# Sums of squares of two RMS norms: added on GpSimd instead of TensorE, and half blocks of the products that may be parted in their middle

## The chip, the cores and the metric

The kernel runs on 1 core of a Trainium2 chip. The metric is the time of the device in microseconds (us), the median of 3 runs; less is better. TensorE is PE in the profile, its weight loads are PEld, VectorE is DVE, ScalarE is ACT, GpSimd is POOL, SyncE (which issues most DMAs) is SP.

## What is computed

One step of a decoder layer, for 1024 prompt tokens and 32 sample tokens that share all weights (1056 columns in all). The part that the change touches comes after the mixer's recurrences and ahead of the MLP:

```python
h = h + rmsnorm(merged @ w_out, norm_mix_post)
xa = cross_attend(rmsnorm(h, norm_xa_pre), mk, mv, xa_wq, xa_wo)
h = h + rmsnorm(xa, norm_xa_post)
ff = square(relu(rmsnorm(h, norm_mlp_pre) @ mlp_w1)) @ mlp_w2
h = h + rmsnorm(ff, norm_mlp_post)

def rmsnorm(x, g):       # x: tokens x 1024, all in float32
    return x * rsqrt(mean(x * x, -1) + 1e-6) * g
def cross_attend(xn, k, v, w_q, w_o):   # 4 heads of 256, 256 memory tokens
    q = xn @ w_q
    return softmax(q . k / 16) . v @ w_o
```

## The kernel before

The last block of the program (`back`) holds features on the 128 partitions (8 blocks of 128 features) and tokens along the free axis, in three chunks of 288, 384 and 384 tokens, in this order. It multiplies by four 1024x1024 matrices in turn (`BackProducts`): the mixer's last branch, w_out, xa_wq, xa_wo. That makes 12 stretches (matrix, chunk), numbered kk = 0 to 11, each of 8 products; a product is two halves of 12 matmuls, since each float32 factor is split into a high and a low part and three of the four partial products are taken (4 input blocks x 3). The high part of a half's weights is made by ACT (`high`, L3163), the low part by DVE (`low`, L3169), three halves ahead.

Two norms follow each of the stretches kk = 3, 4, 5 (w_out) and kk = 9, 10, 11 (xa_wo): `BackNorms`. Here these six are called norm chunks 0 to 5; chunks 0 and 3 have 288 tokens, the others 384. For each:

- Norm 1: of each of the 8 blocks of the product, ACT copies it out of PSUM (L3329) and squares it into one of two buffers `sq` (L3333); PE multiplies the squares by a matrix of ones, which sums over the 128 features of the block and over the blocks in PSUM (`tensor`, L3368). Then ACT makes 1/sqrt as an Ln (L3340) and an Exp (L3342).
- DVE scales two blocks (L3387, twice) and adds the residual (L3390), four times: that gives the new h.
- Norm 2: ACT squares each block of the new h into one of two buffers `sq2` (L3352), PE sums (`tensor2`, L3375), Ln and Exp again, DVE scales (L3396), ACT and DVE split the result into high and low (L3359, L3404). This runs beside the next stretch's products, or, for chunk 5, beside the first products of the MLP (`BackMlp`, L3810), whose order is: four blocks of weights, each with tokens 768-1055 and then 0-383, then the same four with tokens 384-767, which are chunk 5's.

In the stretches 7 and 8 the attention of the prompt (`PromptAttention`: scores L3459, transposes L3471, mixing L3480) and of the samples (`SampleAttention`: transposes of the keys L3602, scores L3611, mixing L3621) is put between the halves.

The order on each engine is set when the program is written. Each piece of work is a generator that yields the time at which its next instructions are due, by a plan (`BackTimes`: for a half 12 x (0.000417 x tokens + 0.012) us, and some room per stretch), and `weave` always takes the piece that is due first. The engines then run in that order and wait for semaphores. So a position in the order is a position in the plan, and the chip can be ahead of it or behind it.

Of the kernel before, what the change touches and what calls it, by code (L numbers as in the profile page):

```python
# [22 lines left out]
KD = D // P  # L23
# [999 lines left out]
class RwkvMasks:  # L1023
# [32 lines left out]
    def pool(self, pool):  # L1056

        def keep(at, pattern, base, mult):
            pool.affine_select(out=at, in_=at, compare_op=ALU.is_ge, fill=0.0, base=base, pattern=pattern, channel_multiplier=mult)
            return pool.drain()  # L1060

        def blocks(t):
            return t.rearrange("p (a c) -> p a c", c=16)
        yield 1
        pool.wait_ge(self.ones_made, 1)
        keep(blocks(self.within), [[-16, 8], [0, 16]], 0, 1)
        keep(blocks(self.within), [[16, 8], [0, 16]], 15, -1)
# [2057 lines left out]
class BackProducts:  # L3125
# [45 lines left out]
    def multiply(self, pe, ready):  # L3171
        for hu, u, hf, b, raw in self.halves():
            yield self.times.half(hu)
            kk = u // 8
            t0, m = self.times.CHUNKS[kk % 3]
            if b == 0:
                for sem, n in ready[kk][hf]:
                    pe.wait_ge(sem, n)
            pe.wait_ge(self.w_lo, hu + 1)
            if hf == 0 and u >= 2:  # L3180
                pe.wait_ge(self.off[u % 2], u // 2)
            ps = self.bank(u)[:, 0:m]
            for q in range(4):
                for i, (w, x) in enumerate(((self.hi, 0), (self.hi, 1), (self.lo, 0))):
                    last = self.nc.tensor.matmul(ps, w[:, hu % 4, q, :], self.pair[x][:, 4 * hf + q, t0:t0 + m],  # L3185
                                                 start=hf == 0 and q == 0 and i == 0, stop=hf == 1 and q == 3 and i == 2)
            last.then_inc(self.product if hf else self.used, 1)
# [95 lines left out]
class BackNorms:  # L3283


    def __init__(self, k, ctx, products, gains):
        self.k, self.nc, self.pr, self.times, self.pair, self.gains = k, k.nc, products, products.times, products.pair, gains
        S = lambda n: k.sem(f"bn_{n}")
        (self.h_in, self.h_out, self.squared, self.summed, self.squared2, self.summed2, self.rstd1, self.resid, self.rstd2, self.normed, self.n_hi, self.n_lo) = (
            S(n) for n in ("h_in", "h_out", "squared", "summed", "squared2", "summed2", "rstd1", "resid", "rstd2", "normed", "n_hi", "n_lo"))  # L3290
        self.sq, self.sq2 = [ctx.enter_context(k.nc.sbuf_tensor(f"bn_sq{i}", [P, 2, 384], F32)) for i in range(2)]
        self.rstd = ctx.enter_context(k.nc.sbuf_tensor("bn_rstd", [P, 384], F32))

# [25 lines left out]
    def evacuate(self, act, work_free):  # L3319
        for i, s, kk, t, m, end in self.items():  # L3320
            for b in range(8):
                u = 8 * kk + b
                yield self.times.off(u)
                if b == 0:
                    sem, n = work_free[kk]
                    act.wait_ge(sem, n)
                act.wait_ge(self.pr.product, u + 1)
                ps = self.pr.bank(u)[:, 0:m]
                self.nc.scalar.activation(self.work[kk % 2][:, b, 0:m], ps, ACT.Copy)  # L3329
                n = 8 * i + b  # L3330
                if n >= 2:
                    act.wait_ge(self.summed, n - 1)
                self.nc.scalar.activation(self.sq[:, n % 2, 0:m], ps, ACT.Square).then_inc(self.squared, 1)  # L3333
                act.drain().then_inc(self.pr.off[u % 2], 1)

    def scalar(self, act):
        activation = self.nc.scalar.activation
        for i, s, kk, t, m, end in self.items():
            def root(bank, done):
                activation(self.rstd[:, 0:m], bank[:, 0:m], ACT.Ln, bias=self.k.eps[:, 0:1], scale=1.0 / D)  # L3340
                act.drain()
                activation(self.rstd[:, 0:m], self.rstd[:, 0:m], ACT.Exp, scale=-0.5).then_inc(done, 1)  # L3342
            yield end + 3.2
            act.wait_ge(self.summed, 8 * (i + 1))
            root(self.k.bank[5], self.rstd1)
            for q in range(KD):
                yield end + 8.2 + 1.2 * q
                n = 8 * i + q
                act.wait_ge(self.resid, 4 * i + q // 2 + 1)
                if n >= 2:  # L3350
                    act.wait_ge(self.summed2, n - 1)
                activation(self.sq2[:, n % 2, 0:m], self.held[:, q, 0:m], ACT.Square).then_inc(self.squared2, 1)  # L3352
            yield end + 20
            act.wait_ge(self.summed2, 8 * (i + 1))
            root(self.k.bank[4], self.rstd2)
            for j in range(4):
                yield end + 24 + 1.4 * j
                act.wait_ge(self.normed, 4 * i + j + 1)
                activation(self.pair[0][:, 2 * j:2 * j + 2, t], self.work[kk % 2][:, 2 * j:2 * j + 2, 0:m], ACT.Copy).then_inc(self.n_hi, 1)  # L3359

    def tensor(self, pe):
        for i, s, kk, t, m, end in self.items():
            for b in range(8):
                yield self.times.half(2 * (8 * kk + b) + 3) + 0.1
                pe.wait_ge(self.squared, 8 * i + b + 1)
                if b == 0 and i:
                    pe.wait_ge(self.rstd1, i)
                self.nc.tensor.matmul(self.k.bank[5][:, 0:m], self.k.ones[:, :], self.sq[:, b % 2, 0:m], start=b == 0, stop=b == 7).then_inc(self.summed, 1)  # L3368

    def tensor2(self, pe):  # L3370
        for i, s, kk, t, m, end in self.items():
            for q in range(KD):
                yield end + 8.9 + 1.2 * q
                pe.wait_ge(self.squared2, 8 * i + q + 1)
                self.nc.tensor.matmul(self.k.bank[4][:, 0:m], self.k.ones[:, :], self.sq2[:, q % 2, 0:m], start=q == 0, stop=q == KD - 1).then_inc(self.summed2, 1)  # L3375

    def vector(self, dve):
        for i, s, kk, t, m, end in self.items():
# [581 lines left out]
def back(k, pair):  # L3960
# [3 lines left out]
    with ExitStack() as ctx:  # L3964
# [22 lines left out]
        with nc.Block() as block:  # L3987
# [428 lines left out]
```

## Time and profile before

| what | value |
|---|---|
| median of 3 runs | 4138.52 us (4135.79 to 4139.5) |
| profiled execution: its time, its span | 4138.71 us, 4137.0 us |
| mean granted TensorE clock | 0.974 of full speed |
| PE busy | 3865.5 us, 93% |
| DVE, ACT, POOL busy | 2353.3, 1544.9, 149.0 us |

The span is the time from the first to the last recorded instruction; 1.7 us lie around it. Busy shares are means over all stages of the program. For one stage the times of its stretch are to be read. A row of the chain of waits gives what the end waited for at each moment. A matmul's row gives its latency; matmuls overlap, and what one costs in a row of many is seen in the chain or between the starts.

### The profile page before, as it was taken

To read this page: it belongs to the slowest core of one execution; us is meant where nothing else is said; L and a number is where in the kernel's file an instruction comes from. 1 tells how busy PE (TensorE), PEld (TensorE's weight loads), DVE (VectorE), ACT (ScalarE), POOL (GpSimd) and SP (SyncE) were. 2 spreads that over 40 slices of the span, in tenths; PEclk is the share of its full clock that TensorE was granted. 3 is DMA by queue.
4 is the path that set the end of the run, shared out by engine and by line. 5 is a ranking of instruction groups with operands and counts; after the bars stand their busy time and mean duration, and the time that the engine had idled before them with its cause. 6 is when DMAs were issued, how large, how long until landed. Compare 5 with 4: busy or idle time off the path is not lost. (4 is left out here: it accounts for less than half of the span.)

```text
span 4137.0 us, 84913 instructions
## 1 busy us (share of the span) xinstructions
PE 3865.5 (93%) x36062; PEld 3542.4 (86%) x36062; DVE 2353.3 (57%) x4619; ACT 1544.9 (37%) x2873; POOL 149.0 (4%) x167
## 2 busy tenths in 40 slices
PE   8999999999899999889987999979988999999998
PEld 4889999988888888889985777769877889999997
DVE  4445646432378886338877777645643564444446
ACT  3123232232277554335325666544512441111112
POOL 0000000000011111010000000000011000000000
PEclk9999999989999999999998999989999999999999
DMA  5323223233455554545641111052323131111102
GB/s 207 90 87 95 92 86 96 82 98 116 141 152 156 147 150 136 170 140 187 211 160 51 35 37 39 23 175 85 110 87 121 38 112 43 46 42 52 41 31 85
DMA packets 375367, 418.71 MB, mean 101 GB/s; under 512 B 50298, under 2 KB 317100, under 8 KB 374124
## 3 DMA queue, kind: packets, MB, share of 16 engines
q1 hardware_dynamic: 362751, 368.14, 29.1%
q0 software_dynamic: 7632, 27.84, 2.3%
q10 hardware_dynamic: 4608, 17.30, 1.0%
q8 instruction: 287, 4.70, 0.5%
q14 instruction: 89, 0.73, 0.1%
HBM read 289.10 MB, written 121.77 MB: 99 GB/s over the span
## 5 line engine op out<-in xcount | busy, mean ns | idle before, releaser
L245 PE MATMUL bank<-xn_hi,pw_whi 128*128 128x352 f32 (+1 forms) x2184 | 730.2, 334 | 27.0 <-PEq L54 13.9
L245 PE MATMUL bank<-xn_hi,pw_wlo 128*128 128x352 f32 (+1 forms) x2184 | 706.9, 324 | 0.0
L245 PE MATMUL bank<-xn_lo,pw_whi 128*128 128x352 f32 (+1 forms) x2184 | 706.2, 323 | 0.0
L245 PEld LDWEIGHTS bank<-xn_hi,pw_whi 128*128 128x128 f32 (+1 forms) x2184 | 412.9, 189 | 50.1 <-issue 35.2
L245 PEld LDWEIGHTS bank<-xn_lo,pw_whi 128*128 128x128 f32 (+1 forms) x2184 | 414.4, 190 | 3.3 <-issue 2.2
L245 PEld LDWEIGHTS bank<-xn_hi,pw_wlo 128*128 128x128 f32 (+1 forms) x2184 | 412.5, 189 | 1.3
L1789 PE MATMUL bank<-sum_x_hi,pw_whi 128*128 128x352 f32 x768 | 256.2, 334 | 42.1 <-DVE sum_x_lo L1768 27.6
L258 ACT ACTIVATE ring<-bank 128x352 f32<-128x352 f32 (+1 forms) x273 | 125.9, 462 | 446.6 <-PE bank L245 445.8
L3185 PE MATMUL bank<-bx_hi,bp_whi 128*128 128x384 f32 (+1 forms) x768 | 270.2, 352 | 18.0 <-DVE bx_lo L3246 17.0
L3810 PE MATMUL bank<-bx_hi,bp_whi 128*128 128x384 f32 (+1 forms) x768 | 251.2, 327 | 4.7 <-issue 4.7
L3810 PE MATMUL bank<-ml_hidden_hi,bp_whi 128*128 128x384 f32 (+1 forms) x768 | 254.4, 331 | 0.0
L230 DVE TENSOR_TENSOR pw_wlo<-ring,pw_whi 128x1024 fp32r<-128x1024 f32 (+1 forms) x92 | 113.6, 1235 | 244.1 <-ACT pw_whi L223 243.6
L1789 PE MATMUL bank<-sum_x_lo,pw_whi 128*128 128x352 f32 x768 | 252.0, 328 | 0.0
L1789 PE MATMUL bank<-sum_x_hi,pw_wlo 128*128 128x352 f32 x768 | 251.8, 328 | 0.0
L3185 PE MATMUL bank<-bx_lo,bp_whi 128*128 128x384 f32 (+1 forms) x768 | 249.8, 325 | 0.0
L3185 PE MATMUL bank<-bx_hi,bp_wlo 128*128 128x384 f32 (+1 forms) x768 | 249.7, 325 | 0.0
L3810 PE MATMUL bank<-bx_lo,bp_whi 128*128 128x384 f32 (+1 forms) x768 | 248.5, 324 | 0.0
L3810 PE MATMUL bank<-bx_hi,bp_wlo 128*128 128x384 f32 (+1 forms) x768 | 248.1, 323 | 0.0
L3810 PE MATMUL bank<-ml_hidden_hi,bp_wlo 128*128 128x384 f32 (+1 forms) x768 | 247.8, 323 | 0.0
L3810 PE MATMUL bank<-ml_hidden_lo,bp_whi 128*128 128x384 f32 (+1 forms) x768 | 247.6, 322 | 0.0
L3785 ACT ACTIVATE bp_whi<-ring 128x512 fp32r<-128x512 f32 x152 | 92.1, 628 | 394.4 <-PE bank L3810 391.4
L3169 DVE TENSOR_TENSOR bp_wlo<-ring,bp_whi 128x512 fp32r<-128x512 f32 x192 | 131.3, 688 | 147.5 <-ACT bp_whi L3163 146.3
(705 smaller groups left out, 10226.6 us busy)
## 6 DMA issues: line engine op xcount, KB each, us to landing
ring<-in_w_in_dram SPq DMA_DIRECT2D x90, 512.0 KB, 4.8
proj_scratch<-ring SPq DMA_DIRECT2D x66, 528.0 KB, 2.9
m_seg<-acum_scratch SPq DMA_DIRECT2D x32, 512.0 KB, 6.7
ring<-in_mlp_w_dram SPq DMA_DIRECT2D x16, 1024.0 KB, 5.4
ring<-in_mlp_w_dram SPq DMA_DIRECT2D x32, 512.0 KB, 3.5
gates_scratch<-ring SPq DMA_DIRECT2D x24, 528.0 KB, 5.3
merged_scratch<-sum_gate ACTq DMA_DIRECT2D x24, 528.0 KB, 5.0
m_raw<-proj_scratch SPq DMA_DIRECT2D x24, 512.0 KB, 5.9
```

What stands on the lines that cost most here:

```text
L230: self.nc.vector.tensor_tensor(self.lo[:, b % 2, :, 0:n], self.raw[:, b % 2, :, 0:n], self.hi[:, b % 2, :, 0:n], ALU.subtract).then_inc(se ...
L245: last = self.nc.tensor.matmul(ps[0:n, 0:m], w[:, q, 0:n], self.pair[x][:, q, t0:t0 + m], start=q == 0 and j == 0, stop=q == KD - 1 and j ...
L258: self.nc.scalar.activation(self.staging[0:n, b % 2, t0:t0 + m], self.banks[e % len(self.banks)][0:n, 0:m], func).then_inc(self.off, 1)
L1789: last = self.nc.tensor.matmul(self.banks[e % n][:, 0:m], w[:, self.slot(b), q, :], self.pair[x][:, q, t0:t0 + m], start=q == 0 and i == 0 ...
L3169: self.nc.vector.tensor_tensor(self.lo[:, hu % 4, :, :], raw, self.hi[:, hu % 4, :, :], ALU.subtract).then_inc(self.w_lo, 1)
L3185: last = self.nc.tensor.matmul(ps, w[:, hu % 4, q, :], self.pair[x][:, 4 * hf + q, t0:t0 + m], start=hf == 0 and q == 0 and i == 0, stop=h ...
L3785: self.nc.scalar.activation(self.pr.hi[:, hv % 4, :, :], self.raw(hv), ACT.Copy).then_inc(self.w_hi, 1)
L3810: last = self.nc.tensor.matmul(ps, w[:, s, q % 4, :], x[h][:, q, t0:t0 + m], start=q == 0 and j == 0, stop=q == 4 * v.halves - 1 and j == 2)
```

## The change

- `multiply` yields once more in the middle of a half, at the mean of the plan's times of this half and the next, so that other work can stand between 6 matmuls and 6.
- The sums over the blocks go to GpSimd. Of each norm, block 0 is squared into buffer 0 and every other block into buffer 1. After each of the blocks 1 to 6 GpSimd adds buffer 1 to buffer 0; ACT waits for that addition before it squares the next block. Block 7 stays in buffer 1. PE multiplies buffer 0 and buffer 1 by the ones, once each per norm.
- PE's place for norm 2's sums is due once, 17.5 us after the stretch's end in the plan.

```diff
             for q in range(4):
+                if q == 2:
+                    yield (self.times.half(hu) + self.times.half(hu + 1)) / 2
...
-                n = 8 * i + b
-                if n >= 2:
-                    act.wait_ge(self.summed, n - 1)
-                self.nc.scalar.activation(self.sq[:, n % 2, 0:m], ps, ACT.Square).then_inc(self.squared, 1)
+                if b >= 2:
+                    act.wait_ge(self.added, 6 * i + b - 1)
+                elif b == 0 and i:
+                    act.wait_ge(self.summed, i)
+                self.nc.scalar.activation(self.sq[:, min(b, 1), 0:m], ps, ACT.Square).then_inc(self.squared, 1)
...
-                if n >= 2:
-                    act.wait_ge(self.summed2, n - 1)
-                activation(self.sq2[:, n % 2, 0:m], self.held[:, q, 0:m], ACT.Square).then_inc(self.squared2, 1)
+                if q >= 2:
+                    act.wait_ge(self.added2, 6 * i + q - 1)
+                elif q == 0 and i:
+                    act.wait_ge(self.summed2, i)
+                activation(self.sq2[:, min(q, 1), 0:m], self.held[:, q, 0:m], ACT.Square).then_inc(self.squared2, 1)
...
     def tensor(self, pe):
         for i, s, kk, t, m, end in self.items():
-            for b in range(8):
-                yield self.times.half(2 * (8 * kk + b) + 3) + 0.1
-                pe.wait_ge(self.squared, 8 * i + b + 1)
-                if b == 0 and i:
-                    pe.wait_ge(self.rstd1, i)
-                self.nc.tensor.matmul(self.k.bank[5][:, 0:m], self.k.ones[:, :], self.sq[:, b % 2, 0:m], start=b == 0, stop=b == 7).then_inc(self.summed, 1)
+            yield self.times.half(2 * (8 * kk + 7) + 3) + 0.1
+            pe.wait_ge(self.added, 6 * (i + 1))
+            pe.wait_ge(self.squared, 8 * (i + 1))
+            if i:
+                pe.wait_ge(self.rstd1, i)
+            for x in range(2):
+                last = self.nc.tensor.matmul(self.k.bank[5][:, 0:m], self.k.ones[:, :], self.sq[:, x, 0:m], start=x == 0, stop=x == 1)
+            last.then_inc(self.summed, 1)
+
+    def pool2(self, pool):
+        for i, s, kk, t, m, end in self.items():
+            for q in range(1, 7):
+                yield end + 8.7 + 1.2 * q
+                pool.wait_ge(self.squared2, 8 * i + q + 1)
+                if q > 1:
+                    pool.wait_ge(self.added2, 6 * i + q - 1)
+                self.nc.gpsimd.tensor_tensor(self.sq2[:, 0, 0:m], self.sq2[:, 0, 0:m], self.sq2[:, 1, 0:m], ALU.add).then_inc(self.added2, 1)
...
     def tensor2(self, pe):
         for i, s, kk, t, m, end in self.items():
-            for q in range(KD):
-                yield end + 8.9 + 1.2 * q
-                pe.wait_ge(self.squared2, 8 * i + q + 1)
-                self.nc.tensor.matmul(self.k.bank[4][:, 0:m], self.k.ones[:, :], self.sq2[:, q % 2, 0:m], start=q == 0, stop=q == KD - 1).then_inc(self.summed2, 1)
+            yield end + 17.5
+            pe.wait_ge(self.added2, 6 * (i + 1))
+            pe.wait_ge(self.squared2, 8 * (i + 1))
+            for x in range(2):
+                last = self.nc.tensor.matmul(self.k.bank[4][:, 0:m], self.k.ones[:, :], self.sq2[:, x, 0:m], start=x == 0, stop=x == 1)
+            last.then_inc(self.summed2, 1)
...
-                weave(prompt.pool(pool, gate), samples.pool(pool))
+                weave(prompt.pool(pool, gate), samples.pool(pool), norms.pool(pool), norms.pool2(pool))
```

The method `pool` is the same for norm 1: for the blocks b = 1 to 6 it is due at half(2 x (8 kk + b) + 3), waits for the square of block b and adds `sq` buffer 1 to buffer 0.

GpSimd's order in the last block, after the change, from its start to the end of chunk 1's first norm (`bn_sq` is `sq` at L3392, norm 1, and `sq2` at L3383, norm 2):

```order
L3392 TENSOR_TENSOR bn_sq<-bn_sq 128x288
L3456 DMA b_region<-key_scratch 128x2048
L3457 DMA b_region<-out_mem_v_prompt_dram 128x2x1024
L3392 TENSOR_TENSOR bn_sq<-bn_sq 128x288 x5
L3383 TENSOR_TENSOR bn_sq<-bn_sq 128x288 x4
L3392 TENSOR_TENSOR bn_sq<-bn_sq 128x384
L3383 TENSOR_TENSOR bn_sq<-bn_sq 128x288 x2
L3392 TENSOR_TENSOR bn_sq<-bn_sq 128x384 x5
```

Before, only the two DMAs stood there. All 72 additions are new (12 for each chunk), and between the fourth and the fifth addition of chunk 0's norm 2 stands one of chunk 1's norm 1; the same holds for chunks 1, 3 and 4.

PE's order where the sums of chunk 0 stand in stretch 4, first before (here one of chunk 1's norm 1 stands beside two of chunk 0's norm 2):

```order
L3368 MATMUL bank<-bn_sq,ones 128x384
L3375 MATMUL bank<-bn_sq,ones 128x288 x2
L3185 MATMUL bank<-bx_hi,bp_whi 128x384
L3185 MATMUL bank<-bx_lo,bp_whi 128x384
L3185 MATMUL bank<-bx_hi,bp_wlo 128x384
```

and now all that is left of norm 2 there:

```order
L3400 MATMUL bank<-bn_sq,ones 128x288 x2
L3187 MATMUL bank<-bx_hi,bp_whi 128x384
L3187 MATMUL bank<-bx_lo,bp_whi 128x384
L3187 MATMUL bank<-bx_hi,bp_wlo 128x384
```

Counted on PE from a stretch's end: norm 1's pair of sums stands after 18 matmuls of the next stretch; norm 2's pair stands 60 matmuls (5 halves) later for the chunks 0, 1, 3 and 4, 96 matmuls (8 halves) later for chunk 2, and 96 matmuls (four half-length visits of the MLP) later for chunk 5. Before, the 8 sums of norm 2 stood singly, in twos and threes between the halves 4 and 10.

PE's order in the attention (key transposes L3602, now L3628; sample scores L3611, now L3637; both wait for each other through a DVE copy), first before:

```order
L3602 MATMUL bank<-ident,b_region 128x128 x4
L3611 MATMUL bank<-b_region 32x128 x4
L3602 MATMUL bank<-ident,b_region 128x128 x4
L3611 MATMUL bank<-b_region 32x128 x4
L3185 MATMUL bank<-bx_hi,bp_whi 128x384
```

and now, at another place of the same stretch:

```order
L3637 MATMUL bank<-b_region 32x128 x4
L3628 MATMUL bank<-ident,b_region 128x128 x4
L3187 MATMUL bank<-bx_hi,bp_whi 128x384
L3187 MATMUL bank<-bx_lo,bp_whi 128x384
L3187 MATMUL bank<-bx_hi,bp_wlo 128x384
```

From the first scores to the start of stretch 10, the pieces of product matmuls go from 44 to 75, the places where scores directly follow the transposes that they need go from 17 to 9, and all mixing pieces stand apart (two pairs stood together before).

## Rows read from the trace of the kernel before

**Rows 1.** Windows: length, then busy us of PE, PEld, DVE, ACT, POOL; clock.

```profile
2869.07:2912.12 43.05, 42.89 (x226) 39.50 (x225) 23.21 (x40) 22.90 (x48) 0.00 (x0) 1.00 0.19 65
2912.12:2957.26 45.14, 44.77 (x226) 39.45 (x225) 26.23 (x40) 24.76 (x48) 0.00 (x0) 1.00 0.48 157
2995.70:3249.11 253.41, 222.31 (x1541) 186.28 (x1542) 97.80 (x186) 64.39 (x163) 32.85 (x61) 0.97 0.26 85
3337.28:3378.68 41.40, 36.60 (x214) 32.95 (x212) 30.17 (x53) 18.38 (x34) 0.00 (x0) 1.00 0.13 46
```

**Rows 2.** Chain of waits: start, us, what (stretches 3 and 11).

```profile
2854.36 0.48 PE bank L3368 x2
2854.84 3.19 PE bank L3185 x24
...
3332.44 0.65 PE bank L3368 x2
3333.08 4.20 PE bank L3185 x24
```

**Rows 3.** Line L3042, GpSimd's only two-input arithmetic: duration min/median/max.

```profile
L3042 POOL TENSOR_TENSOR m_grow<-m_grow,m_cv x32: 2345/2395/3371, 1184.7 to 1636.1; 128x1024 f32<-128x1024 f32 x32
```

**Rows 4.** Timeline of DVE and POOL at such a place: start, us, instruction.

```profile
1395.76 1.28 DVE L2895 SCALAR_TENSOR_TENSOR m_cv<-m_raw,vec,m_cv 128x1024 f32<-128x1024 f32 x1
1395.93 3.37 POOL L3042 TENSOR_TENSOR m_grow<-m_grow,m_cv 128x1024 f32<-128x1024 f32 x1 [13.47 <-ACT m_grow L2994]
...
1398.53 1.85 DVE L2895 SCALAR_TENSOR_TENSOR m_cv<-m_raw,vec,m_cv 128x1024 f32<-128x1024 f32 x1
```

**Rows 5.** Groups by form: busy us, mean ns; idle before, releaser.

```profile
L3387 DVE SCALAR_TENSOR_TENSOR b_work<-b_work,vec,bn_rstd 128x384 f32<-128x384 f32 x32 | 18.3, 612 | 0.0
L3390 DVE TENSOR_TENSOR b_work<-b_work 128x768 f32<-128x768 f32 x16 | 15.3, 959 | 1.2
L3169 DVE TENSOR_TENSOR bp_wlo<-ring,bp_whi 128x512 fp32r<-128x512 f32 x192 | 131.3, 688 | 147.5 <-ACT bp_whi L3163 146.3
```

**Rows 6.** Timeline of ACT, norm chunks 0, 1 and 2.

```profile
2874.29 0.50 ACT L3340 ACTIVATE bn_rstd<-bank,eps 128x288 f32<-128x288 f32 x1 [1.96 <-PE bank L3368]
2879.15 0.43 ACT L3352 ACTIVATE bn_sq<-b_work 128x288 f32<-128x288 f32 x1
...
2917.66 0.58 ACT L3340 ACTIVATE bn_rstd<-bank,eps 128x384 f32<-128x384 f32 x1 [2.12 <-PE bank L3368]
2923.16 0.51 ACT L3352 ACTIVATE bn_sq<-b_work 128x384 f32<-128x384 f32 x1
2932.48 0.52 ACT L3352 ACTIVATE bn_sq<-b_work 128x384 f32<-128x384 f32 x1 [2.26 <-PE bank L3375]
...
2981.30 0.57 ACT L3340 ACTIVATE bn_rstd<-bank,eps 128x384 f32<-128x384 f32 x1
```

**Rows 7.** Timeline of ACT, norm chunk 5.

```profile
3341.81 0.58 ACT L3340 ACTIVATE bn_rstd<-bank,eps 128x384 f32<-128x384 f32 x1 [2.81 <-PE bank L3368]
3347.68 0.92 ACT L3352 ACTIVATE bn_sq<-b_work 128x384 f32<-128x384 f32 x2
3362.35 0.58 ACT L3340 ACTIVATE bn_rstd<-bank,eps 128x384 f32<-128x384 f32 x1 [0.67 <-PE bank L3375]
```

**Rows 8.** Chain of waits, at the MLP's first product with chunk 5.

```profile
3373.94 4.74 issue
```

**Rows 9.** Window just after that wait (columns as in rows 1).

```profile
3378.70:3380.00 1.30, 1.30 (x4) 1.30 (x5) 1.21 (x3) 0.27 (x1) 0.00 (x0) 0.50 0.00 0
3380.00:3382.00 2.00, 2.00 (x8) 2.00 (x8) 1.37 (x3) 0.26 (x1) 0.00 (x0) 0.57 0.00 0
```

**Rows 10.** Waits of PE, 2995 to 3250: us, times, longest.

```profile
PE bank L3611 <- DVE b_region L3651: 13.8, 18, 0.9
PE bank L3480 <- DVE bx_lo L3510: 3.4, 3, 1.5
```

**Rows 11.** Chain of waits, a half of products among the attention.

```profile
3060.52 2.31 PE bank L3185 x12
```

More of the change, by code:

```diff
@@ L3288, in __init__ @@
         S = lambda n: k.sem(f"bn_{n}")
-        (self.h_in, self.h_out, self.squared, self.summed, self.squared2, self.summed2, self.rstd1, self.resid, self.rstd2, self.normed, self.n_hi, self.n_lo) = (
-            S(n) for n in ("h_in", "h_out", "squared", "summed", "squared2", "summed2", "rstd1", "resid", "rstd2", "normed", "n_hi", "n_lo"))
+        (self.h_in, self.h_out, self.squared, self.added, self.summed, self.added2, self.squared2, self.summed2, self.rstd1, self.resid, self.rstd2, self.normed, self.n_hi, self.n_lo) = (
+            S(n) for n in ("h_in", "h_out", "squared", "added", "summed", "added2", "squared2", "summed2", "rstd1", "resid", "rstd2", "normed", "n_hi", "n_lo"))
         self.sq, self.sq2 = [ctx.enter_context(k.nc.sbuf_tensor(f"bn_sq{i}", [P, 2, 384], F32)) for i in range(2)]
@@ L3343, in scalar @@
             yield end + 3.2
-            act.wait_ge(self.summed, 8 * (i + 1))
+            act.wait_ge(self.summed, i + 1)
             root(self.k.bank[5], self.rstd1)
@@ L3347, in scalar @@
                 yield end + 8.2 + 1.2 * q
-                n = 8 * i + q
                 act.wait_ge(self.resid, 4 * i + q // 2 + 1)
-                if n >= 2:
-                    act.wait_ge(self.summed2, n - 1)
-                activation(self.sq2[:, n % 2, 0:m], self.held[:, q, 0:m], ACT.Square).then_inc(self.squared2, 1)
+                if q >= 2:
[3 more added lines that the diff above has]
+                activation(self.sq2[:, min(q, 1), 0:m], self.held[:, q, 0:m], ACT.Square).then_inc(self.squared2, 1)
             yield end + 20
-            act.wait_ge(self.summed2, 8 * (i + 1))
+            act.wait_ge(self.summed2, i + 1)
             root(self.k.bank[4], self.rstd2)
@@ L3370, in tensor2, with pool @@
+    def pool(self, pool):
+        for i, s, kk, t, m, end in self.items():
+            for b in range(1, 7):
+                yield self.times.half(2 * (8 * kk + b) + 3)
+                pool.wait_ge(self.squared, 8 * i + b + 1)
+                if b > 1:
+                    pool.wait_ge(self.added, 6 * i + b - 1)
+                self.nc.gpsimd.tensor_tensor(self.sq[:, 0, 0:m], self.sq[:, 0, 0:m], self.sq[:, 1, 0:m], ALU.add).then_inc(self.added, 1)
     def tensor2(self, pe):
         for i, s, kk, t, m, end in self.items():
-            for q in range(KD):
-                yield end + 8.9 + 1.2 * q
-                pe.wait_ge(self.squared2, 8 * i + q + 1)
-                self.nc.tensor.matmul(self.k.bank[4][:, 0:m], self.k.ones[:, :], self.sq2[:, q % 2, 0:m], start=q == 0, stop=q == KD - 1).then_inc(self.summed2, 1)
+            yield end + 17.5
[4 more added lines that the diff above has]
+            last.then_inc(self.summed2, 1)
```

## The prediction, made before the result was known

> **What bounds the kernel now.** I read four views. The table of the page first: PE is busy 93% of the span, so what counts is PE's time and what PE waits for; everything that changes lies in the last block. Then the windows cut at the ends of stretches [rows 1]: stretch 4 takes 43.05 us and stretch 5 takes 45.14, with PE busy but for 0.2 to 0.4 us, while the attention (253.41 us) and the MLP's start (41.40 us) hold 31.1 and 4.8 us without PE. Then the chain of waits, for the price of a thing in a full queue: a product of 24 matmuls is 3.19 us with 288 tokens and 4.20 with 384, a norm's sum 0.48 and 0.65 [rows 2]. Last the timelines of ACT and DVE beside the norms, for the time at which squares can be ready. The second set of norm chunks (3, 4) does the same work as the first (0, 1), and I take it to cost the same.
>
> **What goes.** Each norm has 8 sums on PE and keeps 2. Six norm chunks lose 12 sums each: 4 x 12 x 0.65 + 2 x 12 x 0.48 = 42.7 us of PE's time. That would be the gain if PE never waited for the additions. Only norm 1's sums go without a catch: its additions have a product of 4.2 us (3.2 with 288) each to hide behind. In stretch 3 that is 6 x 0.48 = **-2.9 us**.
>
> **What an addition costs.** No row shows one of 384 elements. GpSimd's only two-input arithmetic takes 2.395 us for 1024 [rows 3]. In proportion that is 0.90 us for 384; if nearly all were fixed it could be up to 2.4, but only a small part can be, so my bounds are 0.85 and 1.2. I take 0.95, and 0.72 for 288 elements. The Trainium skill (GPSIMD Engine Reference, section 3.1) states 4497 ns for an fp32 addition of 2048 elements; a line through that and the row would give about 1.08 us here, an estimate, and move the sum below by some 0.8 us per chunk, to about 4144 us.
>
> **It isn't alone.** DVE's L2895 takes 1.28 us by itself. GpSimd's instruction that started beside it took 3.37 us in place of 2.395, about the 1.0 us until DVE's ended; the next L2895, started 0.77 us ahead of GpSimd's end, took 1.85 us [rows 4]. Both read two operands from SBUF; they take turns. The Trainium skill says so too (SBUF — State Buffer, section Who interferes with whom: a DVE instruction with two SBUF inputs contends with a GpSimd one that reads SBUF, and the second to issue blocks fully). By that rule, which speaks against this change, norm 2's additions meet just such instructions; the trace agrees.
>
> Beside norm 2's squares DVE does exactly that work, one after another: per pair of blocks two L3387 of 0.612 and one L3390 of 0.959, 2.18 us, and a weight remainder L3169 of 0.688 now and then [rows 5].
>
> **Chunk 1 (384 tokens, beside stretch 5), from the end E of its stretch (2912.12).** Before, Ln starts at E+5.5 and the second square at E+11.0 [rows 6]. Now PE reaches norm 1's pair after 18 matmuls (3.15), so Ln starts at 3.15 + 1.30 = E+4.45, 1.1 us sooner; squares one and two start at about E+9.1 and E+10.0. From E+9.1 on DVE has three more pairs (6.5) and three remainders (2.1), GpSimd six additions (5.7); in turns they last 14.3 us, to E+23.4, and the eighth square (0.5) ends at E+23.9. PE stands before the pair of norm 2 five halves (10.5) after norm 1's, at E+14.95. It waits 8.95 us. Queued behind the waiting pair are the next halves of the stretch; nothing of PE can pass it.
>
> After a wait like this PE comes back at half speed: after 4.74 us of idleness [rows 8] the granted clock is 0.50 and 0.57, that is 1.2 GHz, for about 3 us, 8 matmuls in 2.00 us where 2.4 GHz gives 11.4 [rows 9]. That adds some 1.4 us. Stretch 5 is then 16 halves x 2.10 = 33.6, four sums 2.6, the wait 8.95 and 1.4: 46.5 against 45.14. **+1.4 us, twice (chunks 1 and 4).**
>
> **Chunk 0 (288 tokens, beside stretch 4).** Before, Ln at E+5.2 and the second square at E+10.1 [rows 6]; now Ln at 3.15 + 0.96 = E+4.1. By the same count, DVE's pairs shorter in proportion (7.2 with the remainders), additions 6 x 0.72 plus one of chunk 1's norm 1, which GpSimd's order puts between them (0.95), the eighth square ends at 8.1 + 7.2 + 5.3 + 0.45 = E+21.0. PE's place is E+14.6: wait 6.4. Stretch 4: 33.6 + 4 x 0.48 + 6.4 + 1.4 = 43.3 against 43.05. **+0.3, twice (chunks 0 and 3).**
>
> **Chunk 2 (beside stretch 6).** Before, norm 2's Ln is at 2981.30, E+24.0 [rows 6], and the attention waits for this norm's end. Now PE's place is E+16.5 and the eighth square again ends near E+23.9, the pair 1.3 us later: Ln at E+25.2, and half a half more of products is left behind it, at the low clock. **+2.0.**
>
> **Chunk 5 (beside the MLP).** The MLP's products with chunk 5 wait for this norm: 4.74 us of idleness [rows 8]. So here a saved sum is worth nothing and each us of delay counts whole. Before, E = 3337.28, Ln at E+4.5, second square done at E+11.3, norm 2's Ln at E+25.1 [rows 7]. Now Ln is where it was. After E+11.3 DVE has three pairs (6.5), the relu squares and remainders of the hidden blocks (about 3.5 by the lengths of like forms) and 1.4 of weights, GpSimd 5.7: done near E+28, the pair E+29.2. That is 4.1 later, and 1.4 for the clock. **+5.5.**
>
> **Attention (stretches 7, 8, and 9).** Where scores follow their own transposes PE waits for DVE's copy: 13.8 us in 18 waits, 0.77 each; 8 of 17 such places go: -6.2. The waits of the mixing, 3.4 us [rows 10], go, since each piece now has 6 matmuls (1.05) or more between: -3.4. Of the six sums of norm 1 in stretch 9 (2.9) 2.0 come through, the rest covered waits. Against that, 31 more pieces: a half entered from small matmuls takes up to 2.31 us [rows 11] instead of 2.10; I take 0.15 of the 0.21: +4.7. **-6.9.** From both sides: -13 (breaks free, copies fully hidden) to 0 (other waits come up).
>
> **Sum.** -2.9 + 2 x 0.3 + 2 x 1.4 + 2.0 + 5.5 - 6.9 = +1.1 us on the profiled execution's 4138.7 us, which is 0.2 us over the median of the runs shown: 4139.5, I say 4139.
>
> **The rivals.**
> - A, the additions don't collide (DVE's pairs finish first, or the ports are seldom both wanted). Then a cycle is square 0.51 + addition 0.95 + 0.1: the eighth square of chunk 1 ends at 10.5 + 6 x 1.56 = E+19.9, wait 4.95, stretch 42.6 (-2.6); chunk 0 ends at E+17.1, wait 2.5, no clock loss, stretch 38.0 (-5.0); chunk 2 -2, chunk 5 +1.1. Sum -2.9 - 10.0 - 5.2 - 2.0 + 1.1 - 6.9 = -25.9: 4113. For it: GpSimd was slowed visibly only in some of 32 cases (median 2395, greatest 3371 [rows 3]). Against: DVE is nearly gapless here.
> - B, slower: GpSimd gets its turn only in DVE's gaps and an addition costs 1.2 us, so each of norm 2's chains is 1.5 us (six times 0.25) longer and PE, from its fixed place in the order on, waits that much more in each of six chunks, +9; and the finer pieces of the attention give 3 in place of 6.9, +4. It decides from the point at which an addition with its turn costs over 1.1 us. 4139.5 + 13 = 4152.
> - C, the change does what it says, PE's sums vanish and the additions are done in time: 4138.7 - 42.7 - 6.9 = 4089. For it: PE is busy all the time in stretches 4 and 5. Against: its place for the pair comes at E+15 while even before the eighth square began at 2932.48, E+20.4 [rows 6].
>
> **How the numbers follow.** About 0.2% (8.3 us) is what can be told from no change. Forecast 0.40, own range 4131 to 4147; A 0.28; C 0.08; B 0.24. So faster 0.36, same 0.40, slower 0.24. With less than 2 in 10 left out, C first, and the bounds of an addition's cost and of the attention at the ends: 4110 to 4154.
>
> **What would show it.** Additions of 384 elements near 0.95 us when alone and 1.3 to 2 beside DVE; L3387 and L3390 lengthened beside them; on PE one wait of 5 to 9 us before each pair of norm 2, released by ACT's square, with the clock at 0.5 behind it; stretches 4 and 5 near 43 and 46.5 us; norm 2's second Ln of chunk 5 over 3 us later after E; fewer waits at the sample scores. I am wrong if stretch 5 takes under 43 us, or if the attention isn't shorter by 3 us or more.

## The result, and the profile after

The changed kernel takes 4152.88 us (median of 8 runs, 4145.69 to 4156.73); the kernel before, run beside it, 4137.85 (8 runs). The ratio is 1.0035 [1.0024, 1.0046]: slower by some 15 us. That is inside the forecast range, but outside the likeliest case's own range of 4131 to 4147: it is where rival B stood (4152).

The page's table shows what happened to PE:

```profile
span 4149.8 us, 84759 instructions
PE 3844.6 (93%) x35918; PEld 3529.0 (85%) x35918; DVE 2382.8 (57%) x4619; ACT 1544.6 (37%) x2873; POOL 239.2 (6%) x239
```

The 72 sums have gone, GpSimd is busy with the 72 additions, and the span is 12.8 us longer. The windows of stretches 4, 5, 7 to 9 and of the MLP's start, columns as in [rows 1] and each cut from the first product of a stretch to the next one's, say where:

```profile
2863.87:2908.12 44.25, 38.69 (x203) 37.58 (x202) 28.85 (x40) 22.98 (x48) 13.05 (x12) 0.92 0.18 63
2908.12:2957.54 49.42, 40.18 (x202) 37.27 (x201) 31.55 (x40) 24.63 (x48) 17.80 (x12) 0.90 0.39 129
2995.64:3249.80 254.16, 226.60 (x1542) 185.63 (x1541) 102.58 (x193) 68.56 (x168) 38.87 (x67) 0.97 0.26 85
3343.30:3390.66 47.36, 34.57 (x202) 32.33 (x201) 33.75 (x53) 18.37 (x34) 7.49 (x6) 0.91 0.16 55
```

Stretch 5 was 45.14 us with a PE that stood for 0.4 us; now it is 49.42, PE stands for 9.2 us of it, and its mean clock is 0.90 in place of 1.00. For the stretches 7 to 9 the same cut of the trace of before gives 258.71 us:

```profile
2990.51:3249.22 258.71, 224.69 (x1557) 188.31 (x1555) 102.46 (x193) 67.55 (x169) 32.85 (x61) 0.97 0.26 84
```

Stretch 4 went from 43.05 to 44.25, the MLP's start from 41.40 (41.2 from the first product's own start, as the table below counts) to 47.4. Between the first products of the same stretches in both traces:

| part of the last block | before | after | difference | forecast |
|---|---|---|---|---|
| stretch 3 | 28.74 | 25.59 | -3.15 | -2.9 |
| stretches 4 and 5 | 88.26 | 93.67 | +5.4 | +1.7 |
| stretch 6 | 33.06 | 38.10 | +5.0 | +2.0 |
| stretches 7, 8, 9 (attention) | 258.71 | 254.16 | -4.6 | -6.9 |
| stretches 10 and 11 | 88.25 | 93.50 | +5.3 | +1.7 |
| MLP's start to its first product with chunk 5 | 41.2 | 47.4 | +6.2 | +5.5 |
| sum | | | +14.1 | +1.1 |

The waits of PE in the last block (us in total, times, longest) name the line:

```profile
PE bank L3400 <- ACT bn_sq L3356: 40.9, 6, 8.2
...
PE bank L3637 <- DVE b_region L3677: 7.5, 11, 0.9
...
PE bank L3187 <- ACTq L3337: 1.9, 4, 0.7
```

L3400 is norm 2's pair of sums: six waits, 40.9 us, almost as much as the 42.7 us of sums that left PE. L3637 is the sample scores, 13.8 us in 18 waits before [rows 10], 7.5 in 11 now.

What the pair waits for is seen in GpSimd's and ACT's timelines beside chunk 1 (E is 2908.12; start, us, instruction, idle before and releaser). GpSimd, additions of norm 2 with one of norm 1 (L3392) among them:

```profile
2918.84 1.39 POOL L3383 TENSOR_TENSOR bn_sq<-bn_sq 128x384 f32<-128x384 f32 x1 [12.28 <-ACT bn_sq L3356]
...
2926.38 1.30 POOL L3392 TENSOR_TENSOR bn_sq<-bn_sq 128x384 f32<-128x384 f32 x1
2927.64 1.70 POOL L3383 TENSOR_TENSOR bn_sq<-bn_sq 128x384 f32<-128x384 f32 x1
2930.04 0.99 POOL L3383 TENSOR_TENSOR bn_sq<-bn_sq 128x384 f32<-128x384 f32 x1 [0.69 <-ACT bn_sq L3356]
```

ACT, which answers to [rows 6]:

```profile
2912.76 0.58 ACT L3343 ACTIVATE bn_rstd<-bank,eps 128x384 f32<-128x384 f32 x1 [1.71 <-PE bank L3373]
...
2920.33 0.53 ACT L3356 ACTIVATE bn_sq<-b_work 128x384 f32<-128x384 f32 x1 [1.56 <-POOL bn_sq L3383]
...
2931.12 0.52 ACT L3356 ACTIVATE bn_sq<-b_work 128x384 f32<-128x384 f32 x1 [1.16 <-POOL bn_sq L3383]
```

Each square waits for the addition that frees its one buffer, and each addition for a square: a ring of two engines. The addition of norm 1, for chunk 2, stands in GpSimd's order between the fourth and the fifth of norm 2, and the fifth starts only behind it. Alone (the last one) an addition is 0.99 us; beside DVE the others here take 1.2 to 1.7. From Ln to the start of the eighth square it is 18.4 us; before it was 14.8 (2932.48 less 2917.66 [rows 6]), and PE then had sums to do meanwhile. Now it stands:

```profile
2884.27 2.26 PE L3400 MATMUL bank<-bn_sq,ones 128*128 128x288 f32 x4 [5.56 <-ACT bn_sq L3356]
...
2931.79 2.90 PE L3400 MATMUL bank<-bn_sq,ones 128*128 128x384 f32 x4 [8.18 <-ACT bn_sq L3356]
```

The pair takes 2.90 us in place of the 1.3 that two sums cost in a full queue, because it runs at a lower clock (1.53 us at the full one, in e_warm). The windows behind both waits (length, PE busy and count, granted clock, DMA):

```profile
2884.20:2886.00 1.80, 1.73 (x5) 0.50 0.99 357
...
2890.00:2892.00 2.00, 2.00 (x13) 0.95 0.00 0
2931.70:2934.00 2.30, 2.21 (x5) 0.50 1.02 321
...
2936.00:2938.00 2.00, 2.00 (x8) 0.51 0.93 320
2938.00:2940.00 2.00, 2.00 (x13) 1.00 0.00 0
```

After 5.56 and after 8.18 us without a matmul PE runs at 1.2 GHz (0.50) for about 6 us, then at 2.4: 3 us lost each time. The forecast had taken 3 us at that clock, from [rows 9]. The length of the wait doesn't decide it. The trace of before has a wait of 2.97 us too (in stretch 9, ended at 3191.62), and behind it PE is at the lower clock for 5.8 us; and behind the same 4.74 us as in [rows 9] the changed kernel stays there for 4.7 us. The windows, first before and then now:

```profile
3191.60:3193.50 1.90, 1.12 (x4) 0.50 0.00 0
...
3195.50:3197.50 2.00, 2.00 (x10) 0.53 0.00 0
```

```profile
3390.66:3392.66 2.00, 2.00 (x6) 0.50 0.00 0
...
3394.66:3396.66 2.00, 2.00 (x11) 0.82 1.00 318
```

(PE's time in the table of the page hides the clock: a busy PE at half speed counts as busy.)

Last, DVE beside those additions, against [rows 5]:

```profile
2919.28 1.50 DVE L3169 TENSOR_TENSOR bp_wlo<-ring,bp_whi 128x512 fp32r<-128x512 f32 x1
2920.70 1.89 DVE L3413 SCALAR_TENSOR_TENSOR b_work<-b_work,vec,bn_rstd 128x384 f32<-128x384 f32 x2
```

Alone they are 0.69 and 1.14 us. Both sides pay for the turns.

### The profile page after: what moved, and what is told of

It reads as the page before. It is cut to its first block and busy times, and to the rows that moved or that the text cites. A ratio compares the mean times of both kernels' runs of the same rounds, so it can differ in the third digit from the quotient of the medians.

```text
span 4149.8 us, 84759 instructions
## 1 busy us (share of the span) xinstructions
PE 3844.6 (93%) x35918; PEld 3529.0 (85%) x35918; DVE 2382.8 (57%) x4619; ACT 1544.6 (37%) x2873; POOL 239.2 (6%) x239
## 5 line engine op out<-in xcount | busy, mean ns | idle before, releaser
L3187 PE MATMUL bank<-bx_hi,bp_whi 128*128 128x384 f32 (+1 forms) x768 | 266.6, 347 | 21.8 <-DVE bx_lo L3248 16.8
L3187 PE MATMUL bank<-bx_lo,bp_whi 128*128 128x384 f32 (+1 forms) x768 | 252.6, 329 | 0.0
L3187 PE MATMUL bank<-bx_hi,bp_wlo 128*128 128x384 f32 (+1 forms) x768 | 252.1, 328 | 0.0
L3169 DVE TENSOR_TENSOR bp_wlo<-ring,bp_whi 128x512 fp32r<-128x512 f32 x192 | 143.0, 752 | 157.3 <-ACT bp_whi L3163 156.1
```

The lines of the kernel that those rows point to most:

```text
L3169: self.nc.vector.tensor_tensor(self.lo[:, hu % 4, :, :], raw, self.hi[:, hu % 4, :, :], ALU.subtract).then_inc(self.w_lo, 1)
```

## The experiments

All were timed in five rounds. e_split, e_norm1, e_norm2 and e_late shared one set of runs of the kernel before (4137.87 us), e_n1split, e_dve2, e_late2 and e_half another (4136.84), e_warm, e_ends and e_write a third (4137.03). Ratios are to that kernel.

### The three parts of the change apart

**e_split**: the kernel before, with the halves parted only.

```
+                if q == 2:
+                    yield (self.times.half(hu) + self.times.half(hu + 1)) / 2
```

> The kernel before with the yield in the middle of a half alone; both norms as before. Theory (waits before norm 2's pair of sums are what makes the changed kernel slower; the parting of halves is a small gain): stretches 7 to 9 shorter by 2 to 5 us, everything else as before, 4134 to 4137 us. Rival (the finer pieces are what costs, by 30 more entries of 0.1 to 0.2 us and more): 4141 us or more.

4133.45 us, 0.9989 [0.998, 0.9997]: 4.4 us faster. The finer pieces do cost something. The window of stretches 7 to 9 (length, PE busy and count, clock, DMA) is to be read beside the one of before above:

```profile
2989.12:3245.51 256.39, 229.87 (x1556) 0.97 0.26 84
```

PE stands for 26.5 us in place of 34.0, and at the same mean clock it is busy for 5.2 us more, where the forecast put 4.7 for the finer pieces. So these stretches are only 2.3 us shorter. In the waits the sample scores fall as forecast, and others rise:

```profile
PE bank L3473 <- DVE b_region L3500: 9.3, 6, 3.4
PE bank L3613 <- DVE b_region L3653: 7.5, 11, 0.9
...
PE bank L3461 <- ACTq L3446: 4.0, 1, 4.0
```

The first of these had 5.7 us in 3 waits before, the last 2.9: a wait removed at one place partly came back at another. That is why the forecast's 9.6 us of waits saved came to 7.5.

**e_norm1**: norm 1's six middle squares added by GpSimd, norm 2 as before, no parting.

```
-            for b in range(8):
-                yield self.times.half(2 * (8 * kk + b) + 3) + 0.1
...
+            yield self.times.half(2 * (8 * kk + 7) + 3) + 0.1
+            pe.wait_ge(self.added, 6 * (i + 1))
...
+    def pool(self, pool):
...
-                weave(prompt.pool(pool, gate), samples.pool(pool))
+                weave(prompt.pool(pool, gate), samples.pool(pool), norms.pool(pool))
```

> The changed kernel with norm 2's sums back on TensorE as before and without the parting of halves: only norm 1's additions are on GpSimd. Theory: six sums less per chunk, 2 x 6 x 0.48 + 4 x 6 x 0.65 = 21 us of PE, less what the additions lose where DVE's norm 2 work stands beside them (one took 4.1 us): 12 to 20 us faster than before, 4118 to 4126 us. Rival (norm 1's additions, starved beside DVE and blocking it, cost a large part of the 15 us): within 5 us of before.

4118.92 us, 0.9951 [0.9939, 0.9964]: 18.9 us faster. Stretches 4 and 5 take 83.31 us (88.26 before). The two traces differ by 19.9 us: 15.9 of it lies in the last block up to the MLP's first product with chunk 5, and 4.1 ahead of stretch 3, where the code is the same, so that part isn't the change's.

**e_norm2**: norm 2's only.

```
-            for q in range(KD):
-                yield end + 8.9 + 1.2 * q
...
+            yield end + 17.5
+            pe.wait_ge(self.added2, 6 * (i + 1))
...
-                weave(prompt.pool(pool, gate), samples.pool(pool))
+                weave(prompt.pool(pool, gate), samples.pool(pool), norms.pool2(pool))
```

> The changed kernel with norm 1's sums back on TensorE as before and without the parting of halves: only norm 2's additions are on GpSimd. Theory: PE waits 3 to 8 us before each of the six pairs and comes back at a low clock; 12 to 25 us slower than before, 4150 to 4163 us, and chunk 5's norm ends 4 to 6 us later after its stretch's end. Rival (norm 2's waits only take the place of others): within 5 us of before.

4158.26 us, 1.0046 [1.0033, 1.006]: 20.4 us slower. Its waits:

```profile
PE bank L3386 <- ACT bn_sq L3353: 31.6, 6, 8.1
```

So norm 2's additions are what makes the change slower. But the parts don't add up: -18.9 + 20.4 - 4.4 is -2.9, and together they gave +15. (In the last block of the traces alone it is -15.9 + 20.3 - 4.1 = +0.3 against +14.1.) Stretches 4 and 5 show why: 83.31 us with norm 1 alone, 93.16 with norm 2 alone, 93.67 with both. Once norm 2's chain sets the stretch's end, taking norm 1's sums off PE only brings PE to the pair sooner, and it waits longer there (40.9 against 31.6 us in all). The eighth square of chunk 1 ends 23.6 us after the stretch's end in e_norm2 and 23.5 in the changed kernel.

**e_n1split**: norm 1's additions and the parting, norm 2 on PE (e_norm1 and e_split in one).

> Norm 1's additions on GpSimd, norm 2's sums on TensorE as before, and halves that may be parted. If the two gains (18.9 us of norm 1 alone, 4.4 us of the parting alone) are independent: 4111 to 4117 us, the fastest so far. If the parting's gain lies where norm 1's does (the stretches 4 to 6 were shortened by it too): 4118 us, the same as norm 1 alone.

4118.66 us, 0.9956 [0.9943, 0.997]. Together with e_norm1 it is the fastest of the kernels that leave nothing out; both beat the kernel before and the changed one. The median is where the expectation put it if the parting adds nothing to norm 1's gain; whether it adds a few us these runs can't tell.

### Is it PE's place, or the chain?

**e_late**: the changed kernel with the pair 9.5 us later in PE's order, for the chunks beside products.

```
-            yield end + 17.5
+            yield end + (17.5 if i % 3 == 2 else 27)
```

> The changed kernel with PE's place for norm 2's pair of sums moved 3.5 halves later for chunks 0, 1, 3 and 4 (due 27 in place of 17.5 us after the end in the plan). Theory (PE stands before the pair too early): the waits of 5.56 and 8.18 us fall to 0 and about 1.5, the low clock behind them goes: 25 to 32 us less than the changed kernel, 4121 to 4128 us. Rival (the norm's chain through DVE and GpSimd is the limit wherever PE waits for it): under 8 us less.

4165.78 us, 1.007 [1.0057, 1.0083]: slower still, and my theory of then, that a later place would hide the wait, fell. Waits of PE, and the timeline of PE and ACT:

```profile
PE bank L3187 <- ACTq L3337: 36.8, 13, 5.7
```

```profile
2937.48 0.66 PE L3187 MATMUL bank<-bx_hi,bp_whi 128*128 128x384 f32 x1 [5.68 <-ACTq L3337]
2947.99 0.41 PE L3187 MATMUL bank<-bx_hi,bp_whi 128*128 128x384 f32 x1 [2.67 <-ACTq L3337]
```

```profile
2945.36 0.58 ACT L3343 ACTIVATE bn_rstd<-bank,eps 128x384 f32<-128x384 f32 x1 [7.31 <-PE bank L3400]
```

In these four chunks PE no longer waits at the pair but for a free bank. The copies of the products out of PSUM (L3331) stand in ACT's order behind norm 2's squares and its Ln, and those wait for the chain, or for the pair.

**e_late2**: the same, with norm 2's Ln and Exp moved behind the pair's new place as well.

```
-            yield end + 20
+            yield end + (20 if i % 3 == 2 else 27.9)
```

> As the kernel with the pair of sums 3.5 halves later, and ACT's Ln and Exp of norm 2 moved behind it too (due 27.9 in place of 20 us) for chunks 0, 1, 3 and 4. There ACT had stood before that Ln (7.31 us in chunk 1) with copies out of PSUM behind it, for which PE waited. Theory now (PE waits for ACT, which stands in its order before squares and before the Ln): of the bank waits, 3.77 and 5.68 us (behind the squares) stay, 2.51 and 2.67 us (behind the Ln) go, and there is no wait at the pair: 4134 to 4145 us, less than the changed kernel. Rival (the norm's chain costs the same wherever PE meets it): 4150 us or more.

4155.53 us, 1.0046 [1.0033, 1.0058], which isn't told apart from the changed kernel. The Ln's share is gone (10 us), and the rest stays:

```profile
PE bank L3187 <- ACTq L3337: 18.9, 4, 5.7
PE bank L3187 <- DVE bp_wlo L3169: 12.2, 11, 2.1
```

The wait moves from the pair to the bank and to the weights' remainders. ACT and DVE, slowed by the chain, serve PE's products too, so PE met it at either place of the pair: in stretches 4 and 5 it stands for 14.8 us in the changed kernel and for 14.9 here.

### What makes the chain long

**e_dve2**: the changed kernel with norm 2's additions on DVE.

```
-                self.nc.gpsimd.tensor_tensor(self.sq2[:, 0, 0:m], self.sq2[:, 0, 0:m], self.sq2[:, 1, 0:m], ALU.add).then_inc(self.added2, 1)
+                self.nc.vector.tensor_tensor(self.sq2[:, 0, 0:m], self.sq2[:, 0, 0:m], self.sq2[:, 1, 0:m], ALU.add).then_inc(self.added2, 1)
```

> The changed kernel with norm 2's six additions on DVE in place of GpSimd, due at the same times; norm 1's stay on GpSimd. An addition there takes about 0.56 us (the like L3840 of before) and nobody takes turns with it, but DVE now waits for ACT's squares in its order. Theory (norm 2's chain is DVE's work, the additions and the turns in series): six times 0.4 to 0.8 us less per chain, so the waits before the pairs shrink by 2 to 4 us in each of six chunks, 4130 to 4143 us. Rival (it is the chain of squares and additions with one buffer whatever engine adds, and DVE's waits in its order cost what the turns did): 4148 us or more.

4152.6 us, 1.0037 [1.0024, 1.0049], the same as the changed kernel. The addition itself is 0.62 us there on the mean and 0.56 alone, but DVE now stands up to 0.65 us for the square ahead of it. Waits at the pair:

```profile
PE bank L3400 <- ACT bn_sq L3356: 41.7, 6, 7.9
```

**e_half**: the changed kernel with norm 2's additions over half of the columns; the other half's sums of blocks 1 to 6 are left out.

```
-                self.nc.gpsimd.tensor_tensor(self.sq2[:, 0, 0:m], self.sq2[:, 0, 0:m], self.sq2[:, 1, 0:m], ALU.add).then_inc(self.added2, 1)
+                self.nc.gpsimd.tensor_tensor(self.sq2[:, 0, 0:m // 2], self.sq2[:, 0, 0:m // 2], self.sq2[:, 1, 0:m // 2], ALU.add).then_inc(self.added2, 1)
```

> The changed kernel with norm 2's additions on half of the columns only, so that half of the tokens miss blocks 2 to 7 or so of their sums. A dose: each addition about 0.45 us shorter alone. Theory (the additions stand in series in the chain that ends before PE's pair): each of six chains 3 to 5 us shorter, 4124 to 4136 us. Rival (the chain is set by DVE's residuals and ACT's order, the additions lie beside them): 4147 us or more.

4141.69 us, 1.001 [1.0001, 1.0019], 11 us less than the changed kernel; between the two expectations, and as far from one as from the other (5.7 us over the theory's, 5.3 under the rival's). The additions are shorter by less than half, and so are the waits:

```profile
L3383 POOL TENSOR_TENSOR bn_sq<-bn_sq 128x192 f32<-128x192 f32 x24 | 21.5, 894 | 69.4 <-ACT bn_sq L3356 69.4
...
PE bank L3400 <- ACT bn_sq L3356: 31.1, 6, 6.1
```

**e_write**: the changed kernel with norm 2's additions replaced by a GpSimd instruction that only writes the same buffer; the sum of blocks 1 to 6 is left out. The ring of waits stays, with no operand read from SBUF.

```
-                self.nc.gpsimd.tensor_tensor(self.sq2[:, 0, 0:m], self.sq2[:, 0, 0:m], self.sq2[:, 1, 0:m], ALU.add).then_inc(self.added2, 1)
+                self.nc.gpsimd.memset(self.sq2[:, 0, 0:m], 1.0).then_inc(self.added2, 1)
```

> The changed kernel with norm 2's additions replaced by GpSimd writes of a constant of the same 128 x 384 (or 288) elements: the sum of the squares of blocks 1 to 6 is left out. Nothing is read, so no turns with DVE should be taken. Theory (turns between DVE and GpSimd are a large part of the chain): DVE's instructions beside it keep their 0.61, 0.96 and 0.69 us, and the chain is shorter than with half additions (15.9 us from Ln to the eighth square in chunk 1): 4123 to 4138 us. Rival (only the length of GpSimd's instruction counts): by its length on the line of 0.5 us for 192 and 1.0 us for 384 elements, no less than that line gives, 4141 us for one of about 0.5 us.

4118.64 us, 0.9959 [0.9946, 0.9971]: 34 us less than the changed kernel.

```profile
L3383 POOL MEMSET bn_sq<- 128x384 f32 x24 | 10.1, 419 | 72.0 <-ACT bn_sq L3356 72.0
...
PE bank L3400 <- ACT bn_sq L3356: 19.0, 6, 3.9
```

```profile
2908.10 0.58 ACT L3343 ACTIVATE bn_rstd<-bank,eps 128x384 f32<-128x384 f32 x1 [1.71 <-PE bank L3373]
2910.45 1.14 DVE L3413 SCALAR_TENSOR_TENSOR b_work<-b_work,vec,bn_rstd 128x384 f32<-128x384 f32 x2
```

DVE's instructions beside the writes keep 1.14, 0.96 and 0.69 us (one L3416 took 1.60, beside an addition of norm 1). From Ln to the start of the eighth square of chunk 1 it is 13.8 us here, 15.9 in e_half, 18.4 in the changed kernel. The write is shorter than the addition (0.42 against 1.33 us on the mean) and frees DVE of its turns; how the 4.6 us of the chain divide between the two isn't separated. Even so PE waits up to 3.9 us at a pair: what is left of the chain, in which some of the squares now wait for DVE's residuals (L3416), ends after PE's place even with a step of 0.42 us. With norm 2's sums on PE (e_n1split) it is about as long, 13.6 us. No run gave norm 2's squares a third buffer, so that the one buffer is what costs in the ring is read from the rows and not shown by a run of its own.

### The clock

**e_warm**: the changed kernel with 20 to 30 matmuls of ones into bank 5 ahead of each pair, so that PE waits less. They start once norm 1's root has been read from that bank.

```
             yield end + 17.5
+            pe.wait_ge(self.rstd1, i + 1)
+            for x in range((20, 30, 20, 20, 30, 30)[i]):
+                self.nc.tensor.matmul(self.k.bank[5][:, 0:P], self.k.ones[:, :], self.k.ones[:, :], start=True, stop=True)
             pe.wait_ge(self.added2, 6 * (i + 1))
```

> The changed kernel, and PE multiplies the matrix of ones by itself (20 to 30 times, some 4 to 6.5 us, into bank 5, which nobody reads then) ahead of each pair of norm 2's sums, where it waits 5.3 to 8.2 us anyway. No work is taken away. Theory (a part of the loss is the clock: the changed kernel's rows show 0.50 for about 6 us behind the wait of chunk 1): with PE at work before the pair the clock stays at 2.4 GHz there, 3 us less in each of chunks 0, 1, 3 and 4 and 1 to 3 in the others: 4135 to 4142 us. Rival (the waits are the whole loss, the clock comes back by itself at little cost): 4148 us or more.

4138.57 us, 1.0003 [0.9994, 1.0012]: 14 us less than the changed kernel, by giving PE more to do. The wait is filled, and the pair runs at full clock (PE's timeline, in which a float32 matmul of these is two records):

```profile
2924.96 6.86 PE L3399 MATMUL bank<-ones 128*128 128x128 f32 x60
2933.33 1.53 PE L3403 MATMUL bank<-bn_sq,ones 128*128 128x384 f32 x4 [1.51 <-ACT bn_sq L3356]
```

1.53 us against 2.90. Stretches 4 and 5 take 88.03 us against 93.67: 2.8 us for each of the two waits. The chain isn't shorter here (18.4 us from Ln to the eighth square of chunk 1, as before), so this is the clock's cost by itself: without it the change would have been a draw. The mean granted clock says the same of every execution timed: 0.972 to 0.974 in the 11 of e_warm, 0.965 to 0.969 in the 8 of the changed kernel, 0.972 to 0.976 in those of the kernel before.

### The ends of the two sets

**e_ends**: the changed kernel with norm 2 of chunks 2 and 5 back on PE.

```
+            if i % 3 == 2:
+                for q in range(KD):
+                    yield end + 8.9 + 1.2 * q
+                    pe.wait_ge(self.squared2, 8 * i + q + 1)
+                    self.nc.tensor.matmul(self.k.bank[4][:, 0:m], self.k.ones[:, :], self.sq2[:, q % 2, 0:m], start=q == 0, stop=q == KD - 1).then_inc(self.summed2, 1)
+                continue
...
```

(The waits of ACT and GpSimd are changed to match, left out here.)

> The changed kernel with norm 2 of chunks 2 and 5 back on TensorE as before; their norm 1 and all of chunks 0, 1, 3 and 4 stay. Theory (the losses of the chunks are separate and add up): the 5.0 us of stretch 6 and 6.2 us of the MLP's start come back, 4139 to 4145 us. Rival (what chunks 2 and 5 lose is lost to the attention's and the MLP's own waits afterwards): 4148 us or more.

4139.68 us, 1.001 [1.0001, 1.0018]: 13 us less than the changed kernel, by taking back a third of norm 2's additions. In these two chunks a late norm delays the work that needs it (stretch 6 is back at 33.19 us), and a sum saved on a waiting PE brings nothing.

## Where the forecast was right and where its sum fell short, point by point

The mechanism was right and its sum too small: +1.1 forecast, +14.1 in the traces. That the time lies in the stated range is owed to the range's width, which took in rival B, and not to the sum. In the order of the terms:

- **Stretch 3**, norm 1's sums alone: right (-2.9; -3.15). Elsewhere the same saving didn't come through whole: in e_norm1 stretches 4 and 5 lost twelve sums, 7.8 us, and got 4.95 us shorter, with PE standing for 2.5 us of them where it had been 0.5.
- **An addition alone, 0.95 us**: 0.99. **In turns with DVE**: right in kind; on the mean it is 1331 ns, and L3169, L3413, L3416 are lengthened. For chunk 1 the eighth square was forecast to end at E+23.9, it ended at E+23.5 (2931.64 less 2908.12); PE's wait was 8.95 forecast and 8.18 measured, for chunk 0 6.4 and 5.56. This was the hard part of the forecast, and the number held, in part by luck: for chunk 1 it left out the addition of norm 1 that stands among norm 2's (1.30 us, above), which it had counted for chunk 0, and against that the additions and DVE's work took less time together than one after another.
- **The clock, 1.4 us a wait: the step that failed.** I read how long PE stays at 1.2 GHz after a wait from a single one in the trace of before, of 4.74 us, and took it for waits of 5 to 9 us. After those it is some 6 us, and costs 3. The same trace would have warned me: behind its wait of 2.97 us it is 5.8 us. In stretches 4 and 5 that is 2 x 1.6 = 3.2 us of the 3.7 by which the term was short, in stretches 10 and 11 3.2 of 3.6. In e_warm the filled waits gave 14 us back over six chunks, 2.3 each, where the forecast charged 1.4 for each of five (for chunk 2 only a part of 0.8): about 7 us of the 13 that were missing.
- **Chunk 2, +2.0**: +5.0. I moved its Ln by 1.2 us, and it moved by 5.7: from 2981.30 to 2987.07, with the stretch's start within 0.1 us of the same time. The eighth square ended at E+24.4, half a us later than I said, which is the small part of it; but in ACT's order a weight part (L3163) stands ahead of the Ln, and it waits for PE's products, which run at the lower clock behind the wait at the pair (5.34 us here):

```profile
2986.24 0.63 ACT L3163 ACTIVATE bp_whi<-ring 128x512 fp32r<-128x512 f32 x1 [3.75 <-PE bank L3187]
...
2987.07 0.57 ACT L3343 ACTIVATE bn_rstd<-bank,eps 128x384 f32<-128x384 f32 x1
```

  With the wait filled the stretch takes 36.33 us (e_warm), so 1.8 of the 5.0 are the clock's; with norm 2's sums back on PE it is 33.19 us again (e_ends).
- **Chunk 5, +5.5**: +6.2. Right. The chain that ended last (start, us, what) goes from GpSimd's additions to ACT's square to the pair, again at the lower clock, and the idleness of 4.74 us of [rows 8] is still there behind them:

```profile
3364.75 1.62 POOL bn_sq L3383
...
3370.14 0.53 ACT bn_sq L3356
...
3370.81 2.90 PE bank L3400 x4
...
3385.92 4.74 issue
```

- **Attention, -6.9**: -4.6. The sample scores' waits fell by 6.3 us, as forecast, and others grew (e_split): in all PE stands for 6.5 us less (34.0 to 27.6), where 9.6 were forecast. The price of the finer pieces was right (4.7; 5.2 in e_split). It passes my own mark of 3 us or more, but that mark doesn't show what it was meant to: with the parting alone these stretches are 2.3 us shorter, and with norm 1's additions alone, without any parting, 3.6 (255.10 us in e_norm1).
- **Norm 1's sums "go without a catch"**: nearly. In stretch 5 one addition met DVE's normalisation, which runs with no gap there, and ACT's next square waited for it (GpSimd, ACT):

```profile
2948.42 4.11 POOL L3392 TENSOR_TENSOR bn_sq<-bn_sq 128x384 f32<-128x384 f32 x1 [6.24 <-ACT bn_sq L3336]
```

```profile
2952.57 0.49 ACT L3336 ACTIVATE bn_sq<-bank 128x384 f32<-128x384 f32 x1 [1.85 <-POOL bn_sq L3392]
```

  PE lost 0.25 us by it, one of the four waits of the L3187 row above. The longest of them, 0.7 us, ended at 2948.52 and has nothing to do with this addition.

Two slips of the arithmetic change nothing: 4138.7 - 0.2 + 1.1 is 4139.6, and in [rows 4] DVE's instruction ended 1.1 us after GpSimd's had started, not 1.0.

**Of the rivals** B gave the time, 4152, but not wholly by its mechanism. Its turn-taking at 1.2 us or more an addition is there (1.33), yet the chains are no longer than the forecast's; most of the 9 us it set down for them came from the clock instead (7 us, above), and the attention gave 4.6 where it said 3. A fell: the additions do collide, and e_write, where norm 2's additions take no turns (and the instruction is shorter too), comes near A's 4113 with 4118.64. C fell as argued. Stretches 4 and 5 were to be at 43.3 and 46.5 us and were 44.25 and 49.42.

## What to carry to other kernels

A sum taken off the busiest engine is worth its time only if what replaces it is ready when that engine comes by: norm 1's additions, each behind a product of 3 to 4 us, gave 16 to 19 us, norm 2's, a ring of square and addition with one buffer, cost 20. Where a change makes TensorE wait for some us, add what the clock takes afterwards, here up to 3 us a wait, from all such waits in the trace and not from one, and look for the chain's other servants before moving the wait: ACT and DVE carried PE's copies and weights in the same order. For this kernel the version to keep is norm 1 on GpSimd and norm 2 on TensorE (e_norm1, 4118.92 us).

## What the runs showed of the hardware

- The time at 1.2 GHz after a wait was not one number and didn't follow the wait's length: 3.0 us after 4.74 us of idleness [rows 9] and 4.7 us after the same 4.74 in the changed kernel, 5.8 us after 2.97, about 6 us after 5.56 and after 8.18. What decides it isn't resolved here.
- GpSimd and DVE take turns when both read two operands from SBUF, but not evenly. Beside norm 2's L3413, L3416 and L3169 in chunk 1 an addition of 384 elements goes from 0.99 to between 1.2 and 1.7 us, and DVE's L3169 from 0.69 to 1.50. Beside L3430 and L3169, one after another, an addition took 4.11 us, and none of the DVE instructions beside it was longer than alone. The gaps between DVE's instructions are 0.08 us or less in both places, so what lets GpSimd in at the one and not at the other isn't shown. Beside an instruction that only writes, DVE isn't slowed (e_write). The Trainium skill (SBUF — State Buffer, section Who interferes with whom) names the contention of two SBUF readers, and not with one that only writes; the trace agrees. The rule that the prediction took from it, that the second to issue blocks, doesn't fit the 4.11 us, as the trace dates the addition's start: four DVE instructions that started after that addition, the first two of them below, went ahead of it:

```profile
2948.91 0.68 DVE L3169 TENSOR_TENSOR bp_wlo<-ring,bp_whi 128x512 fp32r<-128x512 f32 x1
2949.51 0.95 DVE L3430 TENSOR_TENSOR bx_lo<-b_work,bx_hi 128x768 fp32r<-128x768 f32 x1
```

- Filling a wait with matmuls of no use made the kernel 14 us faster (e_warm).
